# Forgetting attention: the averages of squares as two split products, with their low squares on VectorE

## The chip, the cores and the metric

One NeuronCore of a Trainium2 chip runs the whole program. The metric is the device time of one execution in microseconds; a lower time is better. The core has five engines that run side by side and wait for each other by semaphores: TensorE (matrix products, PE in the profile, its weight loads PEld), VectorE (DVE), ScalarE (ACT), GpSimd (POOL) and SyncE (SP), which here issues the loads of weights.

## The reference, cut to what matters

The program is two models of two layers each over 512 tokens of width 1024. The change touches one place: layer 1 of the first model, the attention with forget gates (16 heads of 64).

```python
def rms_norm(x, g):
    xf = x.astype(jnp.float32)
    y = xf * lax.rsqrt(jnp.mean(xf * xf, axis=-1, keepdims=True) + RMS_EPS)
    return (y * g.astype(jnp.float32)).astype(x.dtype)

def fox_attention(u, w_in, b_f, q_norm_g, k_norm_g, w_out):
    q, k, v, g, fl = jnp.split(u @ w_in, ...)
    q = rms_norm(q.reshape(bn, sn, 16, 64), q_norm_g).transpose(0, 2, 1, 3) * (64 ** -0.5)
    k = rms_norm(k.reshape(bn, sn, 16, 64), k_norm_g).transpose(0, 2, 1, 3)
    log_f = jax.nn.log_sigmoid(fl + b_f)
    f_cum = jnp.cumsum(log_f, axis=1).transpose(0, 2, 1)
    for blk in range(4):                      # 128 queries each
        s = q[:, :, t0:t1] @ k[:, :, :t1]^T + f_cum[t0:t1] - f_cum[:t1]
        p = softmax(where(causal, s, -inf))
        outs.append(p @ v[:, :, :t1])
    return (concatenate(outs) * sigmoid(g)) @ w_out
```

What matters is the mean of 64 squares inside `rms_norm`, taken for each head and token of q and k.

## The kernel before

**Layout and precision.** Activations lie with features on the 128 partitions and the 512 tokens along the free axis, so a tile of 128x512 holds two heads of 64 features: a pair of heads, `hp` = 0 to 7. Weights come in panels of 128x1024 f32 into a ring of four (`ring`), loaded by SyncE. Every panel is split in two: ScalarE writes its rounded high half (`high`, line 2058, type fp32r), VectorE subtracts for the low half (`low`, line 1285). A product with a panel is then three matmuls per 128 rows (high x high, high x low, low x high, lines 669 to 671, 688 to 690 and 730 to 732), of 512 columns each. `prepare(ahead(key))` on ScalarE and VectorE splits the panels up to two behind the one of `key`; three split panels are held.

**A pass.** The loop over d = 0 to 33 in `paired_attention` is software-pipelined: step d handles two blocks of queries of one pair of heads (four steps r = 0 to 3 for a pair, with 512, 384, 256 and 128 keys), and between its own parts every engine calls `fill(d, part)`, which computes the q, k and gate projections of the pair after it: `hp = d // 4 + 1`, `r = d % 4`. A pass below is the four steps in which the q and k of one `hp` (1 to 7) are made.

- TensorE in step d: scores of the step (lines 918 and 921; they wait for the maxima of the step before), `fill(d, 0)` with the panel products (`FOX_FILL`: r = 0 q, r = 1 the last eighth of q and half of k, r = 2 the other half of k, r = 3 the gate), probabilities times v of step d-2 (line 932), transposes of the probabilities of step d-1 (line 947), with `fill(d, 1)` between the two heads' transposes.
- VectorE in step d: bias (line 1713) and maximum (line 1651) for both heads, `fill(d, 0)`, reciprocal (1663) and scaling of the probabilities (1675), `fill(d, 1)`, a copy of transposed probabilities (1682), and once a pass the gating of a finished pair (1734).
- ScalarE in step d: two exponentials (line 2327), `fill(d, 0)`, a copy of transposed probabilities (2339), `fill(d, 1)`.

**The norm of q (z = 0) and k (z = 1).** `raw(hp, z)` on ScalarE evicts the projection (line 2072) and squares it (2362). `norm(hp, z)` on TensorE multiplies the squares with `mean64`, a block matrix of 1/64 (line 957, both operands f32). `root(hp, z)` on ScalarE takes logarithm and exponential of the mean (2100 and 2103). `normed(hp, z)` on VectorE multiplies (1699). The head of the next pass's first step waits for the normed keys (`fox_k`). Where these stand in each engine's own order is written out by hand in `fill`: for z = 0 `raw` in (part 0, r = 1), and `norm`, `root`, `normed` in (part 1, r = 1); for z = 1 `raw` in (part 0, r = 2), the other three in (part 0, r = 3). For hp = 0 all of it is done ahead of the loop, while TensorE works on the projections of v.

Each engine runs its own program strictly in the order written. All of it is one instruction after another; nothing is rescheduled.

Of the kernel before, what the change touches and what calls it, by code (L numbers as in the profile page):

```python
# [6 lines left out]
P = 128  # L7
D = 1024
T = 512
KT = D // P  # L10
# [298 lines left out]
class Ledger:  # L309
# [33 lines left out]
    def at(self, *event):  # L343

        if not self.table:
            return self.sem("unknown"), 1
        name, value = self.table[event]
        return self.sem(name), value


def build(nc, io, table):
# [40 lines left out]
    def const(name, rows=P):  # L392
        c, w = CONST.at[name]
        return C[0:rows, c:c + w]
# [76 lines left out]
    gla_banks = lambda hp: (B[4], B[5], B[2], B[3]) if hp == 0 else (B[6], B[7], B[4], B[5])  # L471
    NF = H[0:FOX_H, 31, :]
    QG = COL[:, 80:81]
    fox_tile = lambda hp, z: H[:, 4 * (hp % 2) + z, :]

    fox_bias = lambda hd: H[:, 20 + hd % 4, :]
# [143 lines left out]
    def tensor_program():  # L620
# [329 lines left out]
        def fox():  # L950
            gemm(("fl",), u_split, ready=lambda k: ("norm_out", "ln", 1, k), idle=10)
            gemm_tok(("fv", 0), 4, 2, 512, ("fv", 0), B[4:8])

            def norm(hp, z):
                bank = gemm_bank(("fnorm", hp, z))
                pe.wait_ge(*at("fox_square", hp, z))
                ins = pe.matmul(bank[:, :], const("mean64"), H[:, 8 + 2 * z, :], start=True, stop=True)
                ins.then_inc(*mark("tensor_fox", "fox_mean", hp, z))

            def first_norms(i):  # L960
                if i == 2:
                    norm(0, 0)
                    norm(0, 1)
            gemm(("fq", 0), u_split)
            gemm(("fk", 0), u_split)
            pe.wait_ge(*at("fv_out", 0, NTB - 1))
            gemm_tok(("fv", 1), 4, 2, 512, ("fv", 1), B[4:8], first_norms)

            def begin(d):
                if d % 4 == 0:  # L970
                    pe.wait_ge(*at("fox_k", d // 4))

            def fill(d, part):

                hp, r = d // 4 + 1, d % 4
                if part == 0 and r == 3 and hp < KT:
                    norm(hp, 1)
                if part == 0 and hp < KT:
                    for name, of, a, b in FOX_FILL[r]:
                        gemm_some((name, hp + of), a, b)  # L980
                if part == 0 and hp == KT + 1 and r == 0:
                    gemm_some(("fox_out", 0), 0, 3, lambda k: ("fox_low", k))
                if part == 0 and hp == KT:
                    if r in (1, 3):
                        busy(B_of(("fg", KT - 2)), 2 if r == 1 else 1)
                    ins = gemm_some(("fg", KT - 1), 2 * r, 2 * r + 2)
                    if r < 3:
                        ins.then_inc(*mark("tensor_fox", "fox_input_free", r))
                if part == 1 and r == 1 and hp < KT:
                    norm(hp, 0)  # L990

            def out_free(d):
                if d % 4 == 0:
                    if d == 0:
                        pe.wait_ge(*at("fv_out", 1, NTB - 1))
                    if d >= 8:
                        pe.wait_ge(*at("fox_mix", d // 4 - 2))
            paired_attention(("fox",), fox_items(), FOX_PROBS, [B[4], B[5]], FOX_SLOTS, begin, fill, out_free)
# [279 lines left out]
    def vector_program():  # L1278
# [407 lines left out]
        def fox():  # L1686
            sem = "vector_fox"
            z, tmp = TMP[0:FOX_H, 0, 0:T], TMP[0:FOX_H, 1, 0:T]
            prepare(ahead(("fl",)))
            softplus_neg(sem, H[0:FOX_H, 30, :], z, tmp, "fl")  # L1690
            v.tensor_tensor_scan(NF, const("ones", FOX_H)[:, 0:1].broadcast_to([FOX_H, T]), H[0:FOX_H, 30, :], 0.0,
                                 ALU.mult, ALU.add).then_inc(*mark(sem, "forget"))
            v.tensor_scalar(QG, vec1("fox_qg"), 0.125, None, ALU.mult).then_inc(*step(sem))
            v.wait_ge(*last(sem))

            def normed(hp, z):
                dst = fox_tile(hp, z)
                v.wait_ge(*at("fox_rms", hp, z))
                v.scalar_tensor_tensor(dst, dst, QG if z == 0 else vec1("fox_kg"), H[:, 9, :], ALU.mult,
                                       ALU.mult).then_inc(*mark(sem, "fox_q" if z == 0 else "fox_k", hp))  # L1700
            prepare(ahead(("fv", 0, 3)))
            prepare(ahead(("fq", 0)))
            prepare(ahead(("fk", 0)))
            prepare(ahead(("fv", 1, 1)))
            normed(0, 0)
            normed(0, 1)
            prepare(ahead(("fv", 1, 3)))

            def bias(i):
                hp, b, e = i // 8, NTB - 1 - (i % 8) // 2, i % 2  # L1710
                part = fox_bias(2 * hp + e)[:, blk(b)]
                v.wait_ge(*at("bias_landed", 2 * hp + e))
                v.tensor_tensor(part, part, const("causal"), ALU.add).then_inc(*step("vector_attention"))
                v.wait_ge(*last("vector_attention"))

            def fill(d, part):
                hp, r = d // 4 + 1, d % 4
                if hp < KT:
                    if part == 0 and r != 2:
                        prepare(ahead((("fq", hp), ("fk", hp), None, ("fg", hp - 1))[r]))  # L1720
                    if (part, r) in ((1, 1), (0, 3)):
                        normed(hp, 1 - part)
                elif part == 0 and r == 0:
                    prepare(ahead(("fg", KT - 1)))
                elif hp == KT and part == 1 and r < 3:
                    for k in (2 * r, 2 * r + 1):
                        input_low(k, M[:, k, :], ("fox_high", k), ("fox_low", k))

            def end(d):
                if d % 4 == 3:  # L1730
                    hp = d // 4
                    v.wait_ge(*at("fox", "product", d))
                    v.wait_ge(*at("fox_gate", hp))
                    v.tensor_tensor(M[:, hp, :], B[6 + hp % 2][:, :], fox_tile(hp, 2), ALU.mult).then_inc(
                        *mark(sem, "fox_mix", hp))
            paired_attention(("fox",), fox_items(), FOX_PROBS, [B[4], B[5]], FOX_SLOTS, bias, fill, end)
            for k in (KT - 2, KT - 1):
                input_low(k, M[:, k, :], ("fox_high", k), ("fox_low", k))
# [310 lines left out]
    def scalar_program():  # L2049
# [299 lines left out]
        def fox():  # L2349
# [8 lines left out]
            def raw(hp, z):  # L2358
                key, tile = ("fk" if z else "fq", hp), fox_tile(hp, z)
                evict(key, tile)  # L2360
                s.wait_ge(*at("evicted", key))
                s.activation(H[:, 8 + 2 * z, :], tile, ACT.Square).then_inc(*mark(sem, "fox_square", hp, z))

            def root(hp, z):
                s.wait_ge(*at("fox_mean", hp, z))
# [6 lines left out]
            def gate(hp):  # L2372
                gt = fox_tile(hp, 2)
                if hp > 1:
                    s.wait_ge(*at("fox_mix", hp - 2))
                evict(("fg", hp), gt, ACT.Exp, scale=-1.0)
                s.wait_ge(*at("evicted", ("fg", hp)))
                s.activation(gt, gt, ACT.Ln, bias=1.0).then_inc(*step(sem))
                s.wait_ge(*last(sem))
                s.activation(gt, gt, ACT.Exp, scale=-1.0).then_inc(*mark(sem, "fox_gate", hp))  # L2380
            raw(0, 0)
            raw(0, 1)
            prepare(ahead(("fv", 1, 1)))
# [3 lines left out]

            def fill(d, part):
                hp, r = d // 4 + 1, d % 4
                if part == 0 and r == 3 and hp < KT:  # L2390
                    root(hp, 1)
                if part == 0 and r == 3 and hp <= KT:
                    gate(hp - 1)
                if hp < KT:
                    if part == 0:
                        if r == 0:
                            prepare(ahead(("fq", hp)))
                        elif r == 1:
                            raw(hp, 0)
                            prepare(ahead(("fk", hp)))  # L2400
                        elif r == 2:
                            raw(hp, 1)
                    elif r == 1:
                        root(hp, 0)
                elif hp == KT and part == 0 and r < 3:
                    if r == 0:
                        prepare(ahead(("fg", KT - 1)))
                    s.wait_ge(*at("fox_input_free", r))
                    for k in (2 * r, 2 * r + 1):
                        input_high(k, M[:, k, :], ("fox_mix", k), ("fox_high", k))  # L2410
# [353 lines left out]
```

## Time and profile before

| | |
|---|---|
| median of 3 runs | 2763.35 us (2762.67 to 2767.46) |
| the profiled execution | 2761.18 us, of it a span of 2759.7 us from the first to the last instruction |
| mean granted TensorE clock | 0.996 of full speed |
| TensorE busy | 2664.1 us (97%), 17218 matmul records |
| VectorE busy | 1625.9 us (59%) |
| ScalarE busy | 1158.3 us (42%) |
| squares, line 2362 | 16 on ScalarE, 632 ns each |
| mean products, line 957 | 32 records (two for each f32 product) of 592 ns on TensorE |
| roots' last step, line 1699 | 16 on VectorE, 746 to 752 ns |

Busy time of a matmul reaches from its start to its modelled end; successive matmuls overlap, so what one costs is read from start to start. The same holds, by less, for ScalarE and VectorE where nothing has to be waited for. The attention loop of the change lies between 646 and 864 us; the mean products ahead of it stand at 633.78, those of the keys in the seven passes follow each other every 27.84 us, from 664.55 to 831.56.

### The profile page before, as it was taken

The numbers are of one execution on the slowest core, as the hardware profiler recorded it, in microseconds if no ns is written. First come the engines' busy times: TensorE is split into PE (matmuls) and PEld (weight loads), VectorE is DVE, ScalarE is ACT, GpSimd is POOL, SyncE is SP. The second block draws the span as 40 slices with busy tenths as digits, with TensorE's granted clock in tenths as the row PEclk, the third lists the DMA queues.
The fourth block names the chain that finished last, engine by engine and source line by source line (L and its number), as shares of the span: only waits on it lengthen the run. The fifth ranks groups of instructions, "written<-read, shape, count | busy, mean of one in ns | idle before, by whom it ended". The sixth has DMA issues, their size and how long they took to land.

```text
span 2759.7 us, 41751 instructions
## 1 busy us (share of the span) xinstructions
PE 2664.1 (97%) x17218; PEld 2110.4 (76%) x17218; DVE 1625.9 (59%) x2919; ACT 1158.3 (42%) x2016; POOL 9.4 (0%) x21
## 2 busy tenths in 40 slices
PE   7999999999999999999998899999999988999998
PEld 6777888877666788886886668888878766788886
DVE  7887546664556865667556755444465577533334
ACT  3744334234555432424546543222355466322222
POOL 0000000000000000000000000000000000000000
PEclk9999999999999999999999999999999999999999
DMA  8364555532221465653230024444433200223322
GB/s 314 115 221 138 188 178 183 176 128 84 77 77 54 145 201 188 197 184 117 100 130 2 3 77 130 135 149 143 145 132 107 77 3 18 84 99 100 98 94 84
DMA packets 92092, 336.40 MB, mean 122 GB/s; under 512 B 10480, under 2 KB 10736, under 8 KB 91776
## 3 DMA queue, kind: packets, MB, share of 16 engines
q1 hardware_dynamic: 86656, 314.87, 34.6%
q10 hardware_dynamic: 3936, 14.64, 1.5%
q0 software_dynamic: 1312, 4.23, 0.5%
q8 instruction: 137, 2.24, 0.3%
q14 instruction: 51, 0.42, 0.0%
HBM read 331.57 MB, written 2.13 MB: 121 GB/s over the span
## 4 chain that ended last, share of the span: by engine, by line
PE 85%; DVE 8%; ACT 6%; issue 2%; DMA 0%; DVEq 0%; SPq 0%; ACTq 0%
PE bank L669 22%; PE bank L671 22%; PE bank L670 22%; PE bank L688 1%; PE bank L689 1%; PE bank L690 1%; PE bank L947 1%; PE bank L932 1%; ACT probs L2327 1%; PE bank L918 1%; PE bank L730 1%; PE bank L731 1%; PE bank L732 1%; PE bank L712 1%; PE bank L714 1%
## 5 line engine op out<-in xcount | busy, mean ns | idle before, releaser
L1285 DVE TENSOR_TENSOR weights_low<-weight_ring,weights_high 128x1024 fp32r<-128x1024 f32 x404 | 494.1, 1224 | 429.6 <-ACT weights_high L2058 429.1
L669 PE MATMUL bank<-in_high,weights_high 128*128 128x512 f32 x1800 | 706.8, 393 | 3.9 <-DVE in_low L1436 2.8
L671 PE MATMUL bank<-in_high,weights_low 128*128 128x512 f32 x1800 | 701.2, 390 | 0.0
L670 PE MATMUL bank<-in_low,weights_high 128*128 128x512 f32 x1800 | 701.1, 389 | 0.0
L2058 ACT ACTIVATE weights_high<-weight_ring 128x1024 fp32r<-128x1024 f32 x404 | 424.8, 1052 | 409.8 <-PE bank L671 310.1
L669 PEld LDWEIGHTS bank<-in_high,weights_high 128*128 128x128 f32 x1800 | 338.2, 188 | 79.0 <-DVE in_low L1436 5.1
L671 PEld LDWEIGHTS bank<-in_high,weights_low 128*128 128x128 f32 x1800 | 338.2, 188 | 71.2
L670 PEld LDWEIGHTS bank<-in_low,weights_high 128*128 128x128 f32 x1800 | 338.4, 188 | 69.6 <-issue 0.7
L669 PE MATMUL bank<-hidden_split,weights_high 128*128 128x512 f32 x896 | 349.5, 390 | 0.0
L670 PE MATMUL bank<-hidden_split,weights_high 128*128 128x512 f32 x896 | 348.6, 389 | 0.0
L671 PE MATMUL bank<-hidden_split,weights_low 128*128 128x512 f32 x896 | 348.6, 389 | 0.0
L1294 DVE CUSTOM_DVE_ANT_0 weight_ring<-weight_ring,silu_c,vectors 128x1024 f32<-128x1024 f32 x192 | 244.5, 1279 | 0.1
L669 PEld LDWEIGHTS bank<-hidden_split,weights_high 128*128 128x128 f32 x896 | 168.2, 188 | 35.6 <-issue 0.5
L670 PEld LDWEIGHTS bank<-hidden_split,weights_high 128*128 128x128 f32 x896 | 168.2, 188 | 35.2 <-issue 0.5
L671 PEld LDWEIGHTS bank<-hidden_split,weights_low 128*128 128x128 f32 x896 | 168.2, 188 | 35.1
L2175 ACT ACTIVATE hidden_split<-tmp 128x512 fp32r<-128x512 f32 x108 | 68.3, 632 | 269.2 <-DVE tmp L1844 200.7
L2072 ACT ACTIVATE tmp<-bank 128x512 f32<-128x512 f32 x68 | 40.7, 598 | 221.5 <-PE bank L671 219.0
L1459 DVE TENSOR_TENSOR hidden_split<-tmp,hidden_split 128x512 fp32r<-128x512 f32 x108 | 74.8, 693 | 75.4 <-ACT hidden_split L2175 75.4
L1346 DVE SCALAR_TENSOR_TENSOR residual<-bank,modulations,residual 128x512 f32<-128x512 f32 x64 | 48.0, 750 | 119.3 <-PE bank L671 119.2
L2327 ACT ACTIVATE probs<-probs,columns 128x256 f32<-128x256 f32 (+4 forms) x144 | 73.7, 513 | 91.9 <-DVE columns L1651 90.1
L2072 ACT ACTIVATE tmp<-bank,vectors 128x512 f32<-128x512 f32 (+1 forms) x65 | 44.7, 688 | 135.2 <-PE bank L671 125.9
L1844 DVE TENSOR_TENSOR tmp<-bank,tmp 128x512 f32<-128x512 f32 x44 | 30.4, 692 | 113.6 <-PE bank L671 113.6
(395 smaller groups left out, 3345.9 us busy)
## 6 DMA issues: line engine op xcount, KB each, us to landing
weight_ring<-stream SPq DMA_DIRECT2D x596, 512.0 KB, 3.4
mixer_out<-cmp ACTq DMA_DIRECT2D x6, 1024.0 KB, 4.9
hidden<-forget_rows POOLq DMA_DIRECT2D x16, 256.0 KB, 3.8
residual<-x ACTq DMA_DIRECT2D x4, 512.0 KB, 8.3
mixer_out<-cmp SPq DMA_DIRECT2D x2, 1024.0 KB, 6.5
out<-mixer_out ACTq DMA_DIRECT2D x4, 512.0 KB, 2.7
constants<-consts ACTq DMA_DIRECT2D x1, 1821.5 KB, 9.8
silu_c<-c ACTq DMA_DIRECT2D x2, 512.0 KB, 4.4
```

Source lines behind the costliest of these rows:

```text
L669: pe.matmul(bank[:, :], WHI[:, z, cols], high, start=(k == 0), stop=False)
L670: pe.matmul(bank[:, :], WHI[:, z, cols], low, start=False, stop=False)
L671: ins = pe.matmul(bank[:, :], WLO[:, z, cols], high, start=False, stop=(k == ktiles - 1))
L1285: v.tensor_tensor(WLO[:, z, :], ring[:, n % RING, :], WHI[:, z, :].bitcast(F32), ALU.subtract).then_inc(*mark("weights_low", "low", n))
L1294: v.tensor_tensor_reduce(w, w, SC[:, :], 1.0, vec1("ada_b", col, col + 1), ALU.mult, ALU.add, MODS[:, col:col + 1]).then_inc(*mark("modula ...
L1346: v.scalar_tensor_tensor(X[:, m, :], B_of(key)[:, :], gcol_[:, m:m + 1], X[:, m, :], ALU.mult, ALU.add).then_inc(*mark("residual", "evicte ...
L1459: v.tensor_tensor(HSPLIT[:, 1, at_, :], tmp, HSPLIT[:, 0, at_, :].bitcast(F32), ALU.subtract).then_inc(*mark("vector_mlp", *event))
L1844: v.tensor_tensor(tmp, B_of(("gup", l, j))[:, :], tmp, ALU.mult).then_inc(*mark("vector_mlp", "evicted", ("gup", l, j)))
L2058: s.activation(WHI[:, i % NSPLIT, :], ring[:, n % RING, :], ACT.Copy).then_inc(*mark("weights_high", "high", n))
L2072: s.activation(dst, view(B_of(key)[:, :]), func, **kw).then_inc(*mark("scalar_evict", "evicted", key))
L2175: s.activation(HSPLIT[:, 0, at_, :], tmp, ACT.Copy).then_inc(*mark("scalar_mlp", *event))
L2327: s.activation(p, p, ACT.Exp, bias=nm, scale=-1.0, accum_out=COL[:, c + 2 + z:c + 3 + z]).then_inc(*mark(sem, *name, "exp", i))
```

## The change

In both forms the mean is the same number. After the change the squares are split like all other operands: ScalarE squares twice, once into f32 and once into a rounded high half (fp32r); VectorE subtracts for the low half (`square_low`); TensorE multiplies both halves with a rounded copy of `mean64` (1/64 is exact), made once by ScalarE. The new tiles lie in parts of `hidden` that are free there. Three things are moved: `norm`, `root` and `normed` for z = 0 go from (part 1, r = 1) to (part 0, r = 2), on ScalarE ahead of `raw(hp, 1)`. `square_low(hp, 0)` stands in (part 0, r = 1) ahead of the panel's low half, `square_low(hp, 1)` in (part 1, r = 2), ahead of the copy of transposed probabilities.

```diff
@@ -471,6 +471,9 @@
     gla_banks = lambda hp: (B[4], B[5], B[2], B[3]) if hp == 0 else (B[6], B[7], B[4], B[5])
     NF = H[0:FOX_H, 31, :]
     QG = COL[:, 80:81]
+    fox_squares = lambda z: H[:, 8 + 2 * z, :]
+    fox_high, fox_low = (lambda z: HSPLIT[:, 1, 9 + z, :]), (lambda z: HSPLIT[:, 1, 11 + z, :])
+    FOX_MEAN = HSPLIT[:, 1, 13, 0:P]
     fox_tile = lambda hp, z: H[:, 4 * (hp % 2) + z, :]
 
     fox_bias = lambda hd: H[:, 20 + hd % 4, :]
@@ -953,8 +956,10 @@
 
             def norm(hp, z):
                 bank = gemm_bank(("fnorm", hp, z))
-                pe.wait_ge(*at("fox_square", hp, z))
-                ins = pe.matmul(bank[:, :], const("mean64"), H[:, 8 + 2 * z, :], start=True, stop=True)
+                pe.wait_ge(*at("fox_mean_split"))
+                pe.wait_ge(*at("fox_square_low", hp, z))
+                pe.matmul(bank[:, :], FOX_MEAN, fox_high(z), start=True, stop=False)
+                ins = pe.matmul(bank[:, :], FOX_MEAN, fox_low(z), start=False, stop=True)
                 ins.then_inc(*mark("tensor_fox", "fox_mean", hp, z))
 
             def first_norms(i):
@@ -973,8 +978,8 @@
             def fill(d, part):
 
                 hp, r = d // 4 + 1, d % 4
-                if part == 0 and r == 3 and hp < KT:
-                    norm(hp, 1)
+                if part == 0 and r > 1 and hp < KT:
+                    norm(hp, r - 2)
                 if part == 0 and hp < KT:
                     for name, of, a, b in FOX_FILL[r]:
                         gemm_some((name, hp + of), a, b)
@@ -986,9 +991,6 @@
                     ins = gemm_some(("fg", KT - 1), 2 * r, 2 * r + 2)
                     if r < 3:
                         ins.then_inc(*mark("tensor_fox", "fox_input_free", r))
-                if part == 1 and r == 1 and hp < KT:
-                    norm(hp, 0)
-
             def out_free(d):
                 if d % 4 == 0:
                     if d == 0:
@@ -1701,6 +1703,13 @@
             prepare(ahead(("fv", 0, 3)))
             prepare(ahead(("fq", 0)))
             prepare(ahead(("fk", 0)))
+
+            def square_low(hp, z):
+                v.wait_ge(*at("fox_square", hp, z))
+                v.tensor_tensor(fox_low(z), fox_squares(z), fox_high(z).bitcast(F32), ALU.subtract).then_inc(
+                    *mark(sem, "fox_square_low", hp, z))
+            square_low(0, 0)
+            square_low(0, 1)
             prepare(ahead(("fv", 1, 1)))
             normed(0, 0)
             normed(0, 1)
@@ -1716,10 +1725,14 @@
             def fill(d, part):
                 hp, r = d // 4 + 1, d % 4
                 if hp < KT:
+                    if part == 0 and r == 1:
+                        square_low(hp, 0)
                     if part == 0 and r != 2:
                         prepare(ahead((("fq", hp), ("fk", hp), None, ("fg", hp - 1))[r]))
-                    if (part, r) in ((1, 1), (0, 3)):
-                        normed(hp, 1 - part)
+                    if part == 0 and r > 1:
+                        normed(hp, r - 2)
+                    if part == 1 and r == 2:
+                        square_low(hp, 1)
                 elif part == 0 and r == 0:
                     prepare(ahead(("fg", KT - 1)))
                 elif hp == KT and part == 1 and r < 3:
@@ -2359,7 +2372,8 @@
                 key, tile = ("fk" if z else "fq", hp), fox_tile(hp, z)
                 evict(key, tile)
                 s.wait_ge(*at("evicted", key))
-                s.activation(H[:, 8 + 2 * z, :], tile, ACT.Square).then_inc(*mark(sem, "fox_square", hp, z))
+                s.activation(fox_squares(z), tile, ACT.Square).then_inc(*step(sem))
+                s.activation(fox_high(z), tile, ACT.Square).then_inc(*mark(sem, "fox_square", hp, z))
 
             def root(hp, z):
                 s.wait_ge(*at("fox_mean", hp, z))
@@ -2378,6 +2392,7 @@
                 s.activation(gt, gt, ACT.Ln, bias=1.0).then_inc(*step(sem))
                 s.wait_ge(*last(sem))
                 s.activation(gt, gt, ACT.Exp, scale=-1.0).then_inc(*mark(sem, "fox_gate", hp))
+            s.activation(FOX_MEAN, const("mean64"), ACT.Copy).then_inc(*mark(sem, "fox_mean_split"))
             raw(0, 0)
             raw(0, 1)
             prepare(ahead(("fv", 1, 1)))
@@ -2387,8 +2402,8 @@
 
             def fill(d, part):
                 hp, r = d // 4 + 1, d % 4
-                if part == 0 and r == 3 and hp < KT:
-                    root(hp, 1)
+                if part == 0 and r > 1 and hp < KT:
+                    root(hp, r - 2)
                 if part == 0 and r == 3 and hp <= KT:
                     gate(hp - 1)
                 if hp < KT:
@@ -2400,8 +2415,6 @@
                             prepare(ahead(("fk", hp)))
                         elif r == 2:
                             raw(hp, 1)
-                    elif r == 1:
-                        root(hp, 0)
                 elif hp == KT and part == 0 and r < 3:
                     if r == 0:
                         prepare(ahead(("fg", KT - 1)))
```

## Rows read from the trace of the kernel before

**Rows 1.** The page, chain that ended last, by engine.
```profile
PE 85%; DVE 8%; ACT 6%; issue 2%; DMA 0%; DVEq 0%; SPq 0%; ACTq 0%
```

**Rows 2.** Chain of waits, 690 to 722: start us, us, engine tile line.
```profile
713.63 0.70 ACT hidden L2100
...
717.87 0.42 DVE probs L1651
...
720.22 1.10 PE bank L957 x2
```

**Rows 3.** Timeline of TensorE: start us, us, engine line operation [idle before, releaser].
```profile
712.56 1.02 PE L957 MATMUL bank<-hidden,constants 128*128 128x512 f32 x2
713.42 0.60 PE L947 MATMUL bank<-constants,probs 128*128 128x128 f32 x4
...
720.22 1.10 PE L957 MATMUL bank<-hidden,constants 128*128 128x512 f32 x2 [0.43 <-ACT hidden L2362]
...
721.39 0.40 PE L689 MATMUL bank<-in_low,weights_high 128*128 128x512 f32 x1
```

**Rows 4.** Timeline of ScalarE, the same pass.
```profile
710.88 0.63 ACT L2362 ACTIVATE hidden<-hidden 128x512 f32<-128x512 f32 x1
711.42 1.04 ACT L2058 ACTIVATE weights_high<-weight_ring 128x1024 fp32r<-128x1024 f32 x1
...
714.35 0.63 ACT L2103 ACTIVATE hidden<-hidden 128x512 f32<-128x512 f32 x1
...
718.84 0.58 ACT L2072 ACTIVATE hidden<-bank 128x512 f32<-128x512 f32 x1
719.45 0.63 ACT L2362 ACTIVATE hidden<-hidden 128x512 f32<-128x512 f32 x1
```

**Rows 5.** Timeline of VectorE, the same pass.
```profile
712.50 1.22 DVE L1285 TENSOR_TENSOR weights_low<-weight_ring,weights_high 128x1024 fp32r<-128x1024 f32 x1 [2.87 <-ACT weights_high L2058]
...
715.01 0.75 DVE L1699 SCALAR_TENSOR_TENSOR hidden<-hidden,columns 128x512 f32<-128x512 f32 x1 [0.43 <-ACT hidden L2103]
715.68 0.68 DVE L1682 COPY probs_T<-bank 128x512 f32<-128x512 f32 x1
...
718.97 0.17 DVE L1663 RECIPROCAL columns<-columns 128x2 f32<-128x2 f32 x1 [0.67 <-ACT probs L2327]
...
719.70 0.55 DVE L1682 COPY probs_T<-bank 128x384 f32<-128x384 f32 x1
```

**Rows 6.** Instructions of line 1459: duration ns min/median/max, first and last start.
```profile
L1459 DVE TENSOR_TENSOR hidden_split<-tmp,hidden_split x108: 691/693/694, 231.2 to 2716.3; 128x512 fp32r<-128x512 f32 x108
```

**Rows 7.** TensorE's timeline, then stretches: length, each engine's busy us, PEclk, DMA share, GB/s.
```profile
127.72 1.98 PE L880 MATMUL bank<-hidden 64*64 64x64 f32 x64 [4.25 <-DVE hidden L1587]
...
1366.66 0.59 PE L671 MATMUL bank<-in_high,weights_low 128*128 128x512 f32 x1
...
1370.03 0.44 PE L670 MATMUL bank<-in_low,weights_high 128*128 128x512 f32 x1
...
128.00:130.00 2.00, 2.00 (x84) 2.00 (x84) 2.00 (x4) 0.00 (x0) 0.00 (x0) 0.50 0.05 16
...
1474.00:1476.00 2.00, 0.69 (x32) 0.59 (x32) 1.87 (x5) 0.23 (x1) 0.00 (x0) 0.98 0.01 4
1476.00:1478.00 2.00, 1.16 (x9) 0.86 (x10) 1.90 (x7) 1.31 (x6) 0.00 (x0) 0.50 0.00 0
...
2206.00:2208.00 2.00, 0.69 (x32) 0.59 (x32) 1.88 (x5) 0.66 (x2) 0.00 (x0) 1.00 0.00 0
```

**Rows 8.** Timelines of ScalarE, TensorE and VectorE ahead of the loop and in its first pass.
```profile
617.66 0.60 ACT L2072 ACTIVATE hidden<-bank 128x512 f32<-128x512 f32 x1 [2.43 <-PE bank L671]
...
633.78 1.88 PE L957 MATMUL bank<-hidden,constants 128*128 128x512 f32 x4
...
635.73 0.40 PE L731 MATMUL bank<-weights_low,in_high 128*128 128x512 f32 x1
...
659.94 0.75 DVE L1699 SCALAR_TENSOR_TENSOR hidden<-hidden,columns 128x512 f32<-128x512 f32 x1
```

## The prediction, made before the kernel was run

> **What bounds the kernel now.** I read the page first, then the chain of waits through one pass of the forgetting attention, then the timelines of TensorE, ScalarE and VectorE over the same pass. The page says that TensorE holds 85% of the chain that ended last and the two vector engines 14% [rows 1], so work taken from TensorE is worth its full time, unless the piece of the chain there lies on another engine. In the attention loop it does: for each pair of heads hp, in steps d = 4(hp-1)+r with r = 0 to 3, the chain goes from the first mean product to ScalarE's logarithm (713.63), by VectorE to the scores' maximum (717.87), by ScalarE again to the keys' square, and comes back to TensorE at the second mean product, 720.22 [rows 2]. There TensorE has stood for 0.43 us, waiting for the keys' square [rows 3]. So at the head of step r = 3 the helpers already end last, by 0.43 us, and anything added to them ahead of that point is paid in full. The pass repeats every 27.84 us, seven times (hp = 1 to 7).
>
> **The products themselves.** A mean product in f32 is two records. The first pair starts at 712.56 and what follows it at 713.42: 0.86 us. The second starts at 720.22; the second panel product starts at 721.39, and such products follow each other in 0.23, so the first of them had its turn at 721.16: 0.94 us [rows 3]. The new form is two products of the panel kind (a rounded high and low part, 128x512), 2 x 0.23 = 0.46 us. Saved: 0.40 for the queries, 0.48 for the keys. Both move: the queries' product goes from between two transposes of step 1 to the head of step 2, the keys' one stays at the head of step 3. Between products of one kind there is nothing to gain or lose beyond that.
>
> **Ahead of the loop** four f32 records (hp = 0) run from 633.78, and the second panel product behind them starts at 635.73, so they take 1.72; four short ones take 0.91: -0.8 us [rows 8]. The new squares, low halves and the copy of the mean matrix there cost nothing: ScalarE stands 2.43 us ahead of its eviction at 617.66 waiting for TensorE [rows 8], the copy is a quarter as wide as a square, and the low halves are due only at 633.78. If that cover were gone it would be some 3 us, once.
>
> **The loop, step 1.** ScalarE squares the queries at 710.88 and begins the panel's high half at 711.42, so one more square costs 0.54 from start to start [rows 4]. The second square would run 711.42 to 712.05 and the high half ends 0.54 later than now, at 713.00. VectorE today starts the panel's low half at 712.50, with that high half [rows 5]. It now first subtracts: the nearest row is the same operation on hidden_split, 128x512, 0.69 us [rows 6]; the bounds are 0.6 (start to start) and 0.75 (the multiplication of [rows 5]). That runs from 712.09 to 712.78, inside the time until the high half comes at 713.0: it costs nothing, and the low half starts 0.54 late. Queued behind it are the reciprocal, the two scalings, the copy of the turned probabilities, the mix and the maxima of step 2. But the multiplication by the root leaves this place: its wait of 0.43 and its 0.67 (715.01 to 715.68) go [rows 5]. Net, VectorE reaches step 2 about 1.10 - 0.54, with the small overlap of unheld instructions, 0.6 us earlier, and so do ScalarE's exponentials. The panel concerned is only used a step of the next pass later, so its half microsecond is hidden; SyncE's loads, POOL's broadcasts of the forget rows and the rings keep their order.
>
> **The loop, step 2: where it costs.** The root of the queries' mean (logarithm and exponential) now stands on ScalarE between the exponentials and the eviction of the keys. It takes 713.63 to 714.35, plus 0.54 until the next may start: 1.26 us [rows 2, 4]. It ran in a hole of step 1 before. Then the eviction (0.61 until the square) and two squares in place of one: +0.54. Then TensorE does not wait for the square but for VectorE's low half of it, +0.69 and 0.04 for the signal. So the start of the keys' product moves by 1.26 + 0.54 + 0.73 - 0.6 = +1.93 us. In the trace's times: exponentials 0.6 earlier, root 718.24, eviction 719.50, squares 720.11 and 720.65 to 721.28, low half 721.32 to 722.01, product 722.15 in place of 720.22. VectorE is not what holds it: the multiplication by the root can start at 719.62, and with its 0.67 and the 0.73 from reciprocal to copy (718.97 to 719.70) [rows 5] it is free at 721.0, just ahead of the squares. It is close, though: half a microsecond more on VectorE would show. TensorE, 0.40 earlier than now, is done with its scores at 719.39 and stands 2.76 us instead of 0.43. The queries' product at the head of step 2 doesn't wait: its low half has been there since 712.8, and TensorE arrives after 713.
>
> Per pass the panel products of step 3 begin 1.93 - 0.48 = 1.45 us later. After that the pass goes by TensorE as before: the copy of step 2's probabilities, which now waits behind the low half, lands near 722.6, while the product that reads it stands behind 24 panel products, 24 x 0.23 = 5.5 us after that; the maxima of step 3 have the same cover. Nothing gives the 1.45 back, because the next pass's chain starts from TensorE's scores. In the first pass VectorE had no wait ahead of its multiplication (659.94 has none) [rows 8], so the 0.6 is missing: about 2.0. Sum: 6 x 1.45 + 2.0 - 0.8 = +9.9 us.
>
> **The clock.** The new hole follows thin products (transposes, 64-row scores). What such lows do is in the trace: after a wait of 4.25 us the granted clock was 0.50, 1.2 GHz (128 to 130); after a stretch in which TensorE was busy 0.69 of 2 us (1474 to 1476) it was 0.50 until 1478; at the same place of the next layer, 2206 to 2208, busy 0.69 as well, it stayed 1.00; and behind the sums of two columns (line 1042) the panel products ran at half speed from 1366.66 [rows 7]. Three of four fell. A fall costs what the matmuls behind it cost more: eight of them were started between 1366.66 and 1370.03, 3.37 us in place of 8 x 0.23 = 1.82: 1.5 us [rows 7]. Those of step 3 are of this kind. The bounds are 0 and 7 x 1.5 = 10.5; by the share of the four lows I take five falls, 7.5 us.
>
> The Trainium skill, "TensorE: Matmul & The Clock Gate", section "HAM oscillation — how this bites in real kernels", describes a loop in which a gap in each pass makes the array start each next burst at half clock, so that it pays each time. The lows at 128 and 1476 agree, the one at 2206 does not; by that rule in full the sum would take all seven.
>
> **Rivals.** (a) *The clock holds.* The same wait, none of the falls: +9.9, which is 2773.3. For it: the low at 2206. (b) *Only the products count, and it gets faster.* If TensorE, not the helpers, came last at the head of step 3, 16 means would give 14 x 0.44 + 0.8 = 7.0 us: 2756.4. It decides only if the low half were ready 2.76 us before my 722.01; against it stands the wait of 0.43 that exists even now [rows 3]. (c) *The root costs nothing.* If what precedes the eviction came so early that the root's 1.26 fitted before it, the move would be 0.67 per pass, less 0.48: 7 x 0.2 + 0.6 (first pass) - 0.8, about +1, 2764.5. Against it: the root stands behind two exponentials in program order, and these come from VectorE's maxima [rows 2]. (d) *More than I count*: VectorE, free only at 721.0 by my reckoning, ends last, or the later keys' multiplication holds the next pass's scores; 1 us a pass more, 2788.
>
> **How the numbers follow.** The profiled execution took 2761.18 us (span 2759.7 and 1.5 around it); the median of the runs shown is 2763.35, 2.2 above. The sum is 2761.18 + 9.9 + 7.5 = 2778.6 on the profiled execution's scale, 2780.8 on the median's. Chances: forecast 0.52, (a) 0.28, (b) 0.05, (c) 0.08, (d) 0.07. The range of 8 in 10 takes (a) with 3 us below it for the unknown durations (0.2 a pass, twice) and seven falls with 3 above 2784: 2770 to 2787. A measurement of this kernel tells about 0.2%, 5.5 us, from no change. Faster by more than that: (b), 0.05; within it: (c) and a little of (a), 0.10; slower: 0.85.
>
> **What would show it.** Right: in the changed profile a wait of TensorE for VectorE's low square of 2.5 to 3 us in seven passes at the head of step 3; none at the head of step 2; the two split products 0.46 us together; a pass of 29.3 us, or 30.8 with a fall; the root between the exponentials and the eviction of the keys. Granted clock 0.50 behind those waits decides between forecast and (a). Wrong: passes of 27.9 or less, or a second TensorE wait at the scores of step 0. The weakest terms are the 0.6 gained in step 1 and the number of falls.

## The result and the profile after

The changed kernel took 2779.97 us (median of 4 runs, 2779.82 to 2780.95). Beside it the kernel before took 2765.26. The ratio is 1.006, 95% interval 1.0048 to 1.0072, so it is slower by 13 to 20 us. The profiled execution has a span of 2778.6 us against 2759.7, 18.9 us more. TensorE's share of the chain fell, those of the others rose:

```profile
span 2778.6 us, 41784 instructions
...
PE 81%; DVE 9%; ACT 7%; issue 2%; DMA 1%; DVEq 0%; ACTq 0%
```

The waits of TensorE between 600 and 880 us (who waits, for whom, total us, times, longest) have a single entry of weight. Before, the same place (the keys' product at the head of step 3) had waits of 0.43 us in six of the seven passes, and none in the first [rows 3].

```profile
PE bank L961 <- DVE hidden_split L1709: 18.8, 7, 2.7
```

One pass of the changed kernel, TensorE:

```profile
718.69 0.50 PE L961 MATMUL bank<-hidden_split 128*128 128x512 f32 x1
719.03 0.39 PE L962 MATMUL bank<-hidden_split 128*128 128x512 f32 x1
719.26 0.40 PE L691 MATMUL bank<-in_high,weights_high 128*128 128x512 f32 x1
...
724.09 0.28 PE L921 MATMUL bank<-hidden 64*64 64x128 f32 x2
...
727.04 0.77 PE L961 MATMUL bank<-hidden_split 128*128 128x512 f32 x1 [2.67 <-DVE hidden_split L1709]
727.61 0.63 PE L962 MATMUL bank<-hidden_split 128*128 128x512 f32 x1
728.04 0.63 PE L691 MATMUL bank<-in_high,weights_high 128*128 128x512 f32 x1
728.46 0.63 PE L692 MATMUL bank<-in_low,weights_high 128*128 128x512 f32 x1
728.89 0.63 PE L693 MATMUL bank<-in_high,weights_low 128*128 128x512 f32 x1
...
730.46 0.40 PE L691 MATMUL bank<-in_high,weights_high 128*128 128x512 f32 x1
```

The queries' product at 718.69 waits for nothing. The keys' one at 727.04 has waited 2.67 us (2.75 in the first pass, 2.67 or 2.68 in the others). Behind it the products start 0.43 apart and take 0.63 each, half speed, until 730.2. The granted clock (the third number from the end) says so by itself; in the first pass, 664 to 668, it held:

```profile
664.00:668.00 4.00, 1.25 (x12) 0.88 (x8) 3.24 (x10) 2.58 (x6) 0.00 (x0) 1.00 0.00 0
...
727.00:731.00 4.00, 3.96 (x11) 3.18 (x12) 1.37 (x7) 2.99 (x7) 1.07 (x2) 0.59 0.34 79
731.00:735.00 4.00, 4.00 (x23) 3.08 (x23) 2.44 (x5) 0.37 (x2) 0.00 (x0) 1.00 0.50 182
```

It fell so in the six other passes, each time just about the keys' product (696, 727, 758, 788, 819 and 850 us). ScalarE and VectorE in the same pass, to be held beside [rows 4, 5]:

```profile
722.00 0.51 ACT L2340 ACTIVATE probs<-probs,columns 128x256 f32<-128x256 f32 x1 [3.53 <-DVE columns L1653]
722.67 0.51 ACT L2340 ACTIVATE probs<-probs,columns 128x256 f32<-128x256 f32 x1
723.18 0.67 ACT L2113 ACTIVATE hidden<-bank,constants 128x512 f32<-128x512 f32 x1
723.88 0.63 ACT L2116 ACTIVATE hidden<-hidden 128x512 f32<-128x512 f32 x1
724.41 0.58 ACT L2085 ACTIVATE hidden<-bank 128x512 f32<-128x512 f32 x1
725.02 0.63 ACT L2375 ACTIVATE hidden<-hidden 128x512 f32<-128x512 f32 x1
725.56 0.61 ACT L2376 ACTIVATE hidden_split<-hidden 128x512 fp32r<-128x512 f32 x1
```

```profile
717.07 0.69 DVE L1709 TENSOR_TENSOR hidden_split<-hidden,hidden_split 128x512 fp32r<-128x512 f32 x1 [2.44 <-ACT hidden_split L2376]
718.02 1.23 DVE L1287 TENSOR_TENSOR weights_low<-weight_ring,weights_high 128x1024 fp32r<-128x1024 f32 x1 [0.26 <-ACT weights_high L2071]
...
724.54 0.75 DVE L1701 SCALAR_TENSOR_TENSOR hidden<-hidden,columns 128x512 f32<-128x512 f32 x1 [1.91 <-ACT hidden L2116]
725.21 0.16 DVE L1665 RECIPROCAL columns<-columns 128x2 f32<-128x2 f32 x1
725.40 0.62 DVE L1677 TENSOR_SCALAR probs<-probs,columns 128x256 f32<-128x256 f32 x2
726.21 0.69 DVE L1709 TENSOR_TENSOR hidden_split<-hidden,hidden_split 128x512 fp32r<-128x512 f32 x1 [0.18 <-ACT hidden_split L2376]
```

Read down the two: ScalarE is idle 3.53 us until the exponentials, then works without a hole to the second square. It does the root (723.18 to 724.41, 1.23 us) between them and the eviction of the keys. VectorE gets to the low half of the keys' squares 0.18 us ahead of its operand, so ScalarE ends last. The queries' low half at 717.07 ran in the time before the panel's high half came; VectorE still had 0.26 us to wait there.

### The profile page after: what moved, and what is told of

Its sections match the earlier page's. It is cut to its first block, busy times and chain, and to the rows that moved or that the text cites. A ratio compares the mean times of both kernels' runs of the same rounds, so it can differ in the third digit from the quotient of the medians.

```text
span 2778.6 us, 41784 instructions
## 1 busy us (share of the span) xinstructions
PE 2666.3 (96%) x17218; PEld 2117.4 (76%) x17218; DVE 1636.4 (59%) x2935; ACT 1164.7 (42%) x2033; POOL 9.4 (0%) x21
## 4 chain that ended last, share of the span: by engine, by line
PE 81%; DVE 9%; ACT 7%; issue 2%; DMA 1%; DVEq 0%; ACTq 0%
PE bank L672 21%; PE bank L673 21%; PE bank L674 21%; PE bank L691 1%; PE bank L950 1%; DVE weights_low L1287 1%; PE bank L921 1%; PE bank L935 1%; PE bank L733 1%; PE bank L734 1%; PE bank L735 1%; PE bank L692 1%; PE bank L693 1%; ACT probs L2340 1%; PE bank L715 1%
```

## The experiments

All are compared with the kernel before, run beside them; its median over 21 runs was 2763.43 us in the first group (e1, e2, e3, e5) and 2763.97 in the second (e4, e6, e7, e8). Single runs of it lie between 2760.1 and 2767.0 us in the first group and between 2758.8 and 2768.6 in the second. The traces show that the clock also falls in other places of the program, in some executions and not in others (before: only at 127.7, 1366.7 and 1475.9, and in the last 7 us; e1: also at 1510, 1537 and 2217, in time from the span's start). Lengths of a pass are therefore given beside the totals: they are read from one keys' square to the next, and where the clock is the same those after the first agree within 0.07 us. The first differs in e5 (27.61) and e6 (27.84).

### e1: the queries' norm back in its old place, the split kept

```diff
-                if part == 0 and r > 1 and hp < KT:
-                    norm(hp, r - 2)
+                if part == 0 and r == 3 and hp < KT:
+                    norm(hp, 1)
...
+                if part == 1 and r == 1 and hp < KT:
+                    norm(hp, 0)
```

(and so for `root` on ScalarE and `normed` on VectorE.)

> The changed kernel, but the queries' mean product, its root and the multiplication stand again where they stood before (part 1 of step 1); the split into two products stays. My theory (the keys' product waits for a sum of ScalarE and VectorE work: root 1.26, second square 0.54, low half and signal 0.73, less 0.6 gained): the 1.26 and the 0.6 both go, the keys' product starts 0.54 + 0.73 = 1.3 us later than before, a pass costs 1.3 - 0.48 = 0.8 us more, TensorE stands about 2.1 us instead of 2.67. Without falls of the clock the time is 5 us above the kernel before, with six falls 14 above. Rival (the extra square and low half alone explain the loss, the order does not matter): a pass as long as in the changed kernel, 15 us above the kernel before.

Measured: 2771.56 us, ratio 1.0034 (1.0021 to 1.0046). A pass takes 28.70 us, 0.87 over the 27.84 of before; 0.8 was expected. The clock fell in one pass only.

```profile
685.30 0.47 PE L961 MATMUL bank<-hidden_split 128*128 128x512 f32 x1 [0.18 <-DVE hidden_split L1712]
...
693.89 0.47 PE L961 MATMUL bank<-hidden_split 128*128 128x512 f32 x1 [1.65 <-DVE hidden_split L1712]
```

TensorE stands 1.65 us for the keys, not 2.1: part of the time is now spent ahead, at the queries' product, which waits 0.18 for its low half and again stands between two groups of transposes. The rival fails: the pass is 0.55 us shorter than the changed kernel's 29.25 at full clock. So both the extra work and the order cost.

### e2: the hole filled with products whose result is overwritten

```diff
                 bank = gemm_bank(("fnorm", hp, z))
+                if hp and z:
+                    busy(bank, 3)
                 pe.wait_ge(*at("fox_mean_split"))
```

> The changed kernel, and in each of the seven passes TensorE does three f32 products of 384 columns of ones into the mean's own bank ahead of the keys' mean product (their result is overwritten), inside its wait. My theory: the hole is filled for some 1.9 us, the clock stays 1.00 there, the keys' product starts when it did, and the time falls by six falls of 1.5, 9 us, below the changed kernel. Rival (the falls cost nothing, or they do not come from the hole): the clock is 0.50 behind the hole as before, or the time stays within 2 us of the changed kernel.

Measured: 2772.01 us, ratio 1.0036 (1.0022 to 1.0049); the span is 2770.6, 8.0 below the changed kernel's. Each held against the kernel before that was run beside it, the two medians stand 8.6 and 14.7 us above, which is 6.1 apart: outside the rival's 2 us, but less than the 9 expected. The loop itself gives the 9, as the passes show; the rest of the program scatters. TensorE's clock is 1.00 over all seven passes:

```profile
664.00:720.00 56.00, 55.32 (x326) 38.85 (x328) 34.38 (x95) 31.70 (x67) 2.15 (x4) 1.00 0.24 76
720.00:780.00 60.00, 58.66 (x370) 41.30 (x370) 35.08 (x98) 35.52 (x77) 2.14 (x4) 1.00 0.22 71
780.00:850.00 70.00, 67.99 (x413) 47.36 (x410) 41.65 (x115) 41.80 (x88) 2.14 (x4) 1.00 0.20 68
```

The filling products start when the bank comes free, after a wait of 0.67, and the keys' product follows them (these two lines are of the pass around 720):

```profile
722.51 2.20 PE L643 MATMUL bank<-constants 128*128 128x384 f32 x6 [0.67 <-ACT hidden L2087]
...
724.51 0.47 PE L963 MATMUL bank<-hidden_split 128*128 128x512 f32 x1
```

It starts 28.70 us behind the first panel product of the pass before (695.81); in the changed kernel, behind a pass without a fall, this is 28.71 (667.55 to 696.26). Each pass takes 29.23 to 29.27 us, as the changed kernel's first (29.25); its others take 30.74 to 30.80. So a fall costs 1.53 us, and products whose result is not used take it away while the keys' product still starts at the same point. The two terms of the sum, wait and clock, are separated by this run.

### e3: the new order alone, with f32 products

```diff
-                pe.wait_ge(*at("fox_square_low", hp, z))
-                pe.matmul(bank[:, :], FOX_MEAN, fox_high(z), start=True, stop=False)
-                ins = pe.matmul(bank[:, :], FOX_MEAN, fox_low(z), start=False, stop=True)
+                pe.wait_ge(*at("fox_square", hp, z))
+                ins = pe.matmul(bank[:, :], const("mean64"), fox_squares(z), start=True, stop=True)
```

(and neither second square nor `square_low`.)

> The new order alone: means of squares by one f32 product again, no second square, no low halves on VectorE, no copy of the mean matrix; the queries' product, root and multiplication stay in step 2. My theory: the root costs 1.26 on ScalarE and the order gains 1.1 to 1.2 on VectorE (wait 0.43, multiplication 0.67), so the keys' product starts 0.1 us later than before and the first pass loses 1.2: 1 to 3 us above the kernel before, no fall of the clock. Rival (the moved root is the cause): TensorE stands 1.7 us or more at the keys' product, 8 us or more above the kernel before.

Measured: 2764.11 us, ratio 1.0006 (0.9997 to 1.0015): no change that can be told. A pass takes 27.90 us, 0.06 over before, and the wait at the keys' product is 0.52 instead of 0.43:

```profile
694.17 1.10 PE L960 MATMUL bank<-hidden,constants 128*128 128x512 f32 x2 [0.52 <-ACT hidden L2367]
```

So the moved root is paid back by the moved multiplication as long as no split stands between: its 1.26 on ScalarE against the 0.43 + 0.67 that VectorE no longer spends ahead of the maxima. With the split the repayment is smaller. By the timelines it is the second square in step 1 that takes the difference: the panel's high half starts 1.06 us behind the first square (715.89 to 716.95) where it was 0.54, and VectorE's low half of the panel waits for it. No run changes that square alone.

### e8: no low half for the keys

```diff
+                if hp and z:
+                    pe.wait_ge(*at("fox_square", hp, z))
+                    ins = pe.matmul(bank[:, :], FOX_MEAN, fox_high(z), start=True, stop=True)
...
-                    if part == 1 and r == 2:
-                        square_low(hp, 1)
```

> The changed kernel, but in the seven passes the keys' mean is taken from the high half alone: no low half of the keys' squares on VectorE and no second product, so that part of the computation is left out. It measures the VectorE leg of the wait. My theory: the keys' product starts 0.69 + 0.04 us earlier and is 0.23 shorter: TensorE stands 1.9 us instead of 2.67, and a pass without a fall takes 29.23 - 0.96 = 28.3 us. Rival (VectorE, busy with the moved multiplication, is what ends last, and the squares are early): the wait falls by more than 1 us. Open in both: whether a hole of 1.9 us still lets the clock fall.

Measured: 2770.35 us, from a single execution, so that the total says little and the passes have to carry the reading. A pass at full clock takes 28.28 to 28.30 us. The leg over VectorE is what was reckoned, 0.69 + 0.04 of wait:

```profile
696.16 0.48 PE L962 MATMUL bank<-hidden_split 128*128 128x512 f32 x1 [1.94 <-ACT hidden_split L2378]
```

The open point came out both ways: the clock fell in every other pass, the first included, so that passes of 29.90 and 28.28 us alternate. The wait is 2.02 us in the first and 1.94 or 1.95 in all others.

```profile
694.00:702.00 8.00, 6.06 (x33) 4.63 (x25) 4.76 (x14) 5.51 (x12) 1.07 (x2) 1.00 0.24 67
723.00:731.00 8.00, 6.54 (x22) 5.26 (x23) 5.04 (x16) 4.81 (x11) 1.07 (x2) 0.79 0.27 73
```

### e5: old place for the queries, the keys' product behind half of the gate's

```diff
+            def late_norm(hp, a):
+                key = ("fnorm", hp, 1)
+                turns.append(key)
+                bank_of[key] = B[len(turns) % 2]
+                before = turns[-3]
+                gemm_some(("fg", hp - 1), 0, a)
+                pe.wait_ge(*at("evicted", before))
+                norm(hp, 1, bank_of[key])
+                gemm_some(("fg", hp - 1), a, KT)
```

(called with a = 4 in step 3; on VectorE `normed(hp, 1)` stands ahead of the panel's low half.)

> Split products, the queries' norm in its old place, and the keys' mean product behind half of the 24 gate products of step 3 (12 matmuls, 2.7 us), so that TensorE has work while the low half is made; VectorE multiplies the keys ahead of the panel's low half. My theory: no wait of TensorE at the keys' product, no fall, and each pass gets the whole saving of the products, 0.40 + 0.48, and the old wait of 0.43: 27.84 - 1.3 = 26.5 us a pass, 9 us below the kernel before. Rival (the helpers are the bound of the whole pass, not of this place): the wait shows up at another product, and the time is within 3 us of the kernel before.

Measured: 2759.79 us, ratio 0.9985 (0.9976 to 0.9994). A pass takes 27.00 us, not 26.5. The wait at the keys' product is gone, but the queries' product, between the transposes, now waits a little each time:

```profile
PE bank L971 <- DVE hidden_split L1722: 1.9, 7, 0.8
```

Of this total 0.85 us is the first pass; the six others wait 0.17 or 0.18. What the place between the transposes costs beyond the wait is read from start to start:

```profile
711.25 0.66 PE L950 MATMUL bank<-constants,probs 128*128 128x128 f32 x4
712.08 0.47 PE L971 MATMUL bank<-hidden_split 128*128 128x512 f32 x1 [0.17 <-DVE hidden_split L1722]
712.38 0.40 PE L972 MATMUL bank<-hidden_split 128*128 128x512 f32 x1
712.62 0.60 PE L950 MATMUL bank<-constants,probs 128*128 128x128 f32 x4
```

```profile
712.07 0.66 PE L947 MATMUL bank<-constants,probs 128*128 128x128 f32 x4
```

From the first transposes to the second it is 1.37 us; in the kernel before, whose first transposes are the last line, it was 1.35 (712.07 to 713.42 [rows 3]). So at this place the split saves nothing: the pair costs 0.54 and not 0.46, and the product starts 0.83 behind the transposes instead of 0.49, of which the wait is 0.17. The expected 0.40 for the queries is missing, and that is nearly all of the 0.5 between 27.0 and 26.5. The rival came true in its first half, a wait at another product, though a small one. In its second it can be neither held nor dropped: the time is 3.6 us below the kernel before, with an interval of 1.7 to 6.6.

### e6: the same place for the keys with f32 products

The edit is that of e5 on the kernel before, with its f32 product.

> The kernel before (f32 mean products, queries' norm in its old place), only with the keys' product behind half of the gate products and VectorE's multiplication of the keys ahead of the low half. My theory: only the old wait of 0.43 goes: a pass of 27.4 us, 3 us below the kernel before, and 3 us above the run with split products in the same place, whose pass took 27.0 (its saving of 0.88 less a wait of 0.27 that it brought). Rival (the split is worth nothing once the place is right): a pass of 27.0 as there.

Measured: 2762.66 us, ratio 0.999 (0.998 to 0.9999). That is 1.3 us below the kernel before where 3 were expected. A pass takes 27.40 us: the old wait of 0.43 has gone, as expected, and the trace has no wait at the mean products in the passes. Against e5 the split is worth 0.40 us a pass of the 0.88 that was reckoned: that of the keys' product, since the queries' saves nothing between the transposes.

### e7: all of the queries' norm later

```diff
+                if part == 0 and r == 2 and hp < KT:
+                    norm(hp, 0)
...
+                    elif r == 2:
+                        root(hp, 0)
```

(`norm` on TensorE in part 0, `root` on ScalarE in part 1, behind the copy; both multiplications on VectorE in step 3, and `late_norm` as in e5.)

> Split products; the queries' product at the head of step 2, its root on ScalarE behind the copies of step 2 and not ahead of the keys' eviction, both multiplications on VectorE in step 3, the keys' product behind half of the gate products. My theory: the wait of 0.27 at the queries' product and the change of product kind around it (0.17) go too, TensorE waits for nothing in a pass: 26.5 us, 9 to 10 us below the kernel before. Rival (VectorE with both multiplications in step 3 is late for the next pass's first scores): a new wait there of 0.5 us or more a pass, not faster than 27.0.

Measured: 2768.13 us, ratio 1.0017 (1.0008 to 1.0027), a pass of 28.19 us: neither theory. The new wait is not where the rival put it either:

```profile
PE bank L691 <- ACT hidden L2126: 11.1, 7, 1.6
```

TensorE stands 1.6 us at the first gate product. The two accumulation banks are used in turn, and `late_norm` takes the keys' turn ahead of the gate's; so the gate's bank is the one that the queries' mean has just occupied, and it comes free with the logarithm of the root (line 2126), which this order puts late. Step 3 begins with that wait, and the clock fell behind it in two of the seven passes, which took 29.8 us.

### e4: the changed kernel's own order, with the keys' product moved

```diff
-                    norm(hp, r - 2)
+                if part == 0 and hp < KT and r == 3:
+                    late_norm(hp, 5)
...
+                    if part == 0 and r > 1:
+                        normed(hp, r - 2)
                     if part == 0 and r != 2:
                         prepare(...)
```

(the first line stays for r = 2; a = 5 puts 15 of the 24 gate products ahead.)

> The changed kernel in its own order (root of the queries ahead of the keys' eviction), only with the keys' mean product behind 15 of the 24 gate products of step 3, 3.4 us, and VectorE's multiplication of the keys ahead of the panel's low half. My theory: the chain of the helpers is as long as in the changed kernel (keys' product possible 2.67 us after TensorE has its scores), but TensorE has 3.4 us of other work there: no wait, no fall, a pass of 26.5 to 26.8 us, 8 to 10 us below the kernel before. Rival: the helpers' delay of 1.9 us comes back at the next pass's first scores, which wait for the multiplied keys: a wait of 1 us a pass there, within 3 us of the kernel before.

Measured: 2752.49 us, ratio 0.9959 (0.9945 to 0.9973), 7 to 15 us faster than the kernel before. The span is 28.0 below the changed kernel's. A pass takes 26.53 us. TensorE has no idle time in the whole of it:

```profile
720.00:780.00 60.00, 60.00 (x381) 42.74 (x380) 39.56 (x111) 39.03 (x83) 3.22 (x6) 1.00 0.25 83
```

Up to the low half of the keys' squares the helpers do the same work in the same order as in the changed kernel, root ahead of the eviction and low half on VectorE:

```profile
715.92 0.67 ACT L2125 ACTIVATE hidden<-bank,constants 128x512 f32<-128x512 f32 x1
716.62 0.63 ACT L2128 ACTIVATE hidden<-hidden 128x512 f32<-128x512 f32 x1
717.16 0.58 ACT L2097 ACTIVATE hidden<-bank 128x512 f32<-128x512 f32 x1
717.77 0.63 ACT L2387 ACTIVATE hidden<-hidden 128x512 f32<-128x512 f32 x1
718.31 0.62 ACT L2388 ACTIVATE hidden_split<-hidden 128x512 fp32r<-128x512 f32 x1
```

```profile
718.96 0.69 DVE L1721 TENSOR_TENSOR hidden_split<-hidden,hidden_split 128x512 fp32r<-128x512 f32 x1 [0.19 <-ACT hidden_split L2388]
```

TensorE has other work until they are done: its keys' product comes at 720.58 in that pass, and the next scores find the multiplied keys ready. This run shows that the loss of the changed kernel comes from the position of the keys' product in TensorE's order. One other operation moved with it: in step 3 VectorE multiplies the keys ahead of the panel's low half. That comes behind the keys' product and can't have shortened the wait of the same pass, but whether the next scores would be in time without it was not run. The run also shows, beside e5, that the head of step 2 is the better place for the queries' product: 26.53 against 27.00, with nothing to wait for in either at the keys'.

## Why the prediction was right, point by point

- **The products.** 0.46 for the new pair holds where it stands among its kind: ahead of the loop four products pass in 0.91, and at the head of step 2 the pair and its change of kind cost 0.57 (718.69 to 719.26), of which 0.09 falls on the panel product in the kernel before. Behind the wait the pair costs 0.54 (667.01 to 667.55, the pass at full clock), so the keys' saving was 0.40 there and not 0.48. In e4 the keys' pair stands among panel products, and the 0.88 a pass show nearly in full: 27.84 - 0.88 - 0.43 is 26.53.
- **Step 1.** The queries' low half at no cost: shown, with 0.26 us left of its cover. The second square at 0.54 (715.89, 716.42, 716.95): measured 0.53 each. The gain of 0.6, called one of the two weakest terms, was 0.69: from the first panel product of step 3 to the second exponential of the next step 2 it is 25.01 us before (693.32, the turn of the first panel product reckoned as in the prediction, to 718.33) and 24.32 in e2 (695.81 to 720.13).
- **Step 2.** Root 1.26: 1.23. Eviction to square 0.61: 0.61. Second square 0.54: 0.54. Low half 0.69 and signal 0.04: 0.69 and 0.04 (squares end at 726.17, low half starts at 726.21). The reckoned wait of 2.76 was 2.67. VectorE is free just ahead of the squares, with 0.18 to spare, as the trace of before allowed one to reckon.
- **The pass.** 1.45 longer was reckoned, 1.41 measured (29.25, with the clock held). Two misses of about 0.1 cancel in it: the keys' product started 1.80 later and not 1.93, and its pair saved 0.40 and not 0.48. e1, e3 and e8 each take out terms of that sum and get 28.70, 27.90 and 28.28; by the sum they should have got 28.6, 27.9 and 28.3.
- **The clock.** Five falls of 1.5 us were forecast, six came, at 1.53 (e2). The size was read from one low; the low at 1476 of the kernel before was twice as long as the prediction says, with the clock still at 0.50 from 1478 to 1482, so a longer fall had to be reckoned with too. The number was a share of four lows, and was right by luck as much as by reason. The falls also come in a row, which the share did not foresee. e8 shows that the length of the wait does not decide alone: nearly equal waits, and the clock falls in every other pass. What the trace of before allows is the statement that such a low can cost 1.5 us.
- **The Trainium skill**, "TensorE: Matmul & The Clock Gate", section "HAM oscillation — how this bites in real kernels", describes a loop that pays for a gap at each round. The gap there is a wait for loads that is longer than the compute of a round, while here TensorE has work in all of the pass but 2.67 us. The changed kernel agrees in six of seven passes, e8 in four of seven, e7 in two, e1 in one.
- **The sum.** 9.9 and 7.5 were 17.4; the span grew by 18.9. By the end of the loop (the last wait for turned probabilities, 863.23 before, 882.84 after) it was 19.6: 1.0 that arose ahead of the first mean product, -0.8 for the four products there, 1.9 in the first pass (2.0 was reckoned), six times 1.40, and six falls, 9.2. The 1.0 (first mean product at 634.76 against 633.78) has nothing to do with the change, since in e2, which has the same program up to there, the product stands at 633.75; 0.7 of it is a fall of the clock near 131 that lasted longer. The remaining -0.7 arose behind the loop.
- **The total.** 2779.97 lies 0.8 from the forecast of 2780.8, closer than the sum deserves. Beside it the kernel before took 2765.26, and not the 2763.35 that the forecast started from: the measured difference is 14.7 us, the forecast one 17.4.
- **Rival (a)**, the clock holds, is what e2 makes by force: 2772.0 against 2773.3. **(b)**, only the products count, needed the helpers to be out of the way; e4 puts them there and gives 2752.5, below the 2756.4 of (b), since the old wait goes as well. **(c)**, the root fits in ahead of the eviction, did not come: it stands between exponentials and eviction with its full 1.23, and e1, which takes it out again, is 0.55 us a pass shorter. With f32 products (e3) it costs next to nothing. **(d)** did not come.

## What to carry to other kernels

When an engine's operation gets cheaper but asks for one more step on its helpers, look where the chain runs at the point where that operation stands: if the helpers already end last there (here by 0.43 us), the added step is paid in full and what was saved ahead of that point only lengthens the wait. An idle hole of 2.67 us on TensorE cost 1.53 us more through its clock in six passes of seven. The remedy here was not less work: put the waiting operation behind work that is ready (here 15 products that needed nothing new), and move as little else as possible. Check then what shares its buffers, since a bank that turns with the order can bring the wait back elsewhere, as in e7.

## What the runs showed of the hardware that was not expected

The falls of the clock follow the rhythm of the passes, and the length of the wait does not say which passes they hit. In the changed kernel a wait of 2.75 us brought no fall in the first pass, and waits of 2.67 one in each of the next six; waits of 1.94 to 2.02 us brought one in every other pass (e8); waits of 1.57 to 1.65 us brought two in seven in e7, and of 1.06 to 1.70 one in seven in e1. Why these passes and not the others stays open. So two kernels with nearly the same hole can differ by several falls, at 1.5 us each, and some of the scatter between executions of one kernel (2758.8 to 2768.6 for the kernel before over 21 runs) goes with the clock: the fastest of these runs has a mean granted clock of 0.998, the slowest 0.991. How much of it comes from where was not measured.
